# Building both layers' filter spectra before the first layer, keeping them in HBM, and reloading them

## The chip, the cores and the metric

One Trainium2 chip (trn2), one core. TensorE multiplies (PE in the profile, PEld its weight loads), VectorE (DVE), ScalarE (ACT) and GpSimd (POOL) do the element-wise work, SyncE (SP) issues most DMAs. The metric is the device time of one execution in microseconds; lower is better.

## The reference, cut to what matters

Two layers, each over 128 context tokens and 512 latent tokens, model width 1024. Each layer mixes tokens by attention and by a long convolution whose filter is made by a small network from position features only:

```python
def hyena_filters(L, lp):
    ...
    h = jnp.sin(lp['filt_freq1'] * (feats @ lp['filt_w1'] + lp['filt_b1']))
    h = jnp.sin(lp['filt_freq2'] * (h @ lp['filt_w2'] + lp['filt_b2']))
    h = (h @ lp['filt_w3']).reshape(L, 2, HY_W)
    return h * window[:, None, :]

def bidir_long_conv(u, h, bias):
    ...
    G = jnp.fft.rfft(g, n=2 * L, axis=0)      # g: the filter, both halves
    y = jnp.fft.irfft(U * G[None], n=2 * L, axis=1)[:, :L]
    return y + u * bias
```

The filter h, and so its spectrum G, depends on the weights alone, not on the tokens. HY_W is 512. After this branch come two gated projections, an output projection, a LayerNorm and a gated feed-forward network.

## The kernel before

**Arithmetic.** Every large product is made of three matmuls of rounded parts: a float32 operand is split into a high part (a copy to fp32r on ScalarE) and a low part (the difference, on VectorE, sometimes on GpSimd), and high*high, high*low and low*high are added in PSUM. "hi" and "lo" in names mean these parts.

**Weights.** SyncE streams them in chunks of up to 128x2048 through two raw buffers (`stream`, the SyncE program L414 to L449). ScalarE makes `w_hi` (L917) and VectorE `w_lo` (L1312) of each chunk. A chunk's DMA starts once the chunk two places earlier has been split. Chunks named F0, F1, I0, I1 are the blocks of the forward and inverse discrete Fourier transforms. Each engine has its own program, run in the order in which it is written; semaphores tie them.

**Prologue** (before layer 0's first product at L563). `ada` (L455) multiplies the conditioning by eight chunks of `ada` weights, in 16 tiles of 128 columns; ScalarE copies the rows out (L891) and TensorE turns them (L494). TensorE turns the input x into columns (L477), and VectorE copies them out (L1253, L1254). The first two filter-network products run (L485, L497); between them VectorE reduces the argument of the sine (`sine_arg`, L1257 to L1271) and ScalarE takes the sine (L898). The second sine's arguments are worked out in layer 0, between the splits of the q, k and v weights. Then ScalarE and GpSimd make the modulated input h and its two parts for each of eight blocks (`h_make` L964, `h_lo` L1772), and TensorE's `opening` (L549, matmul L563) consumes them as they come: first with the first weight chunk, then (L563 again) with the second.

**Layers.** In both layers: q, k, v; rotary; six z chunks interleaved with attention for five token blocks (`qk` L613, `tpv` L628 and L637). VectorE's `o_sb` (L1415) of the fifth block ends the attention. Then comes the filter and spectrum stage, in this order on TensorE:

1. `u_transposed` for four blocks (L653).
2. Ten filter rows (L759): h2T times w3. VectorE multiplies each by its window (L1541), and for each pair of rows adds and subtracts (L1547, L1548), waits for ScalarE's high part (L921), makes the low part itself (L1316), and only then goes on. Four further sums and differences follow (L1557), each with its parts. GpSimd loads the windows in four pieces (L1814).
3. The filter's spectrum: five pairs, `spectrum` (L668) into `aux_psum`, ScalarE copying to `g_spec` (L1082). Pairs 0, 1 and 2 take 12 matmuls each, pairs 3 and 4 take 24.
4. The signal's spectrum for pairs 0 to 2 (L668 into `gemm_psum`), from u blocks copied by ScalarE (L1072), folded by VectorE (L1564) and split.
5. For each pair VectorE multiplies the two spectra (L1577 to L1592) and splits the result (L1316); `inverse` (L680) starts with pair 1, and pairs 3 and 4 alternate with it.

The chunk of F1 is loaded twice per layer, once for step 3 and once for step 5.

## Time and profile before

| | us |
|---|---|
| Median of the runs shown | 2186.02 |
| Lowest and highest of three | 2185.12, 2197.18 |
| The profiled execution | 2192.11 |
| Its span, first to last instruction | 2190.3 |
| TensorE busy | 2066.8 (94% of the span) |
| VectorE busy | 1171.1 (53%) |
| ScalarE busy | 756.8 (35%) |
| GpSimd busy | 167.5 (8%) |

The span is what the trace covers; 1.8 us lie around it. Busy shares are means over stages with different limits. The chain of waits follows the last instruction back to what released it; a row of it is time that the end of the run depended on. The granted clock is the share of full speed that TensorE's clock had: 1.00 is 2.4 GHz and 0.50 is 1.2 GHz.

### The profile page before, as it was taken

Reading aid. Unit: us, or ns where it says so; the run is one execution under the profiler, and the core shown is the slowest. Engines: PE = TensorE matmul, PEld = TensorE weight load, DVE = VectorE, ACT = ScalarE, POOL = GpSimd, SP = SyncE. Lnnn points to the kernel's source line nnn. Section 1 sums busy time; section 2 is a strip of 40 time slices with the busy share of each in tenths; the row PEclk is TensorE's granted clock in tenths of the full one; section 3 lists DMA queues with packets and bytes.
Section 4 is the critical chain, followed back from the end, with each engine's and each line's share of the span. In section 5 each row is a group of like instructions: output and inputs, shape, how many; then the busy total and the mean of one; then the engine's idle time right before and its main releaser. Section 6 shows DMA issues by size and latency. Waiting matters only on the chain.

```text
span 2190.3 us, 30937 instructions
## 1 busy us (share of the span) xinstructions
PE 2066.8 (94%) x13302; PEld 1968.8 (90%) x13302; DVE 1171.1 (53%) x1716; ACT 756.8 (35%) x1114; POOL 167.5 (8%) x183
## 2 busy tenths in 40 slices
PE   7899978999999999999999997899999999999997
PEld 5888857899989999999988885689998999999996
DVE  3353567765566767776454446772335533234335
ACT  1543424522254321333153243452224533123313
POOL 0300000100032000000130000010003300000011
PEclk9999888999999999999999899899999999999999
DMA  6211021343313345433212012111221221222121
GB/s 241 107 68 39 18 87 49 116 139 141 135 58 112 136 151 181 156 141 142 99 53 95 34 37 87 39 61 66 87 77 61 75 77 54 92 77 77 60 67 49
DMA packets 32721, 199.37 MB, mean 91 GB/s; under 512 B 3926, under 2 KB 4487, under 8 KB 14280
## 3 DMA queue, kind: packets, MB, share of 16 engines
q1 hardware_dynamic: 30424, 188.23, 24.2%
q0 software_dynamic: 2160, 9.16, 1.2%
q8 instruction: 105, 1.72, 0.3%
q14 instruction: 32, 0.26, 0.0%
HBM read 194.49 MB, written 2.88 MB: 90 GB/s over the span
## 4 chain that ended last, share of the span: by engine, by line
PE 84%; DVE 7%; ACT 4%; issue 2%; DMA 1%; SPq 0%; POOL 0%; ACTq 0%; DVEq 0%; POOLq 0%
PE gemm_psum L513 49%; PE gemm_psum L543 14%; PE aux_psum L628 3%; PE gemm_psum L563 3%; PE gemm_psum L526 3%; PE gemm_psum L581 3%; PE aux_psum L680 2%; PE aux_psum L613 2%; PE gemm_psum L668 1%; PE aux_psum L668 1%; ACT h_src_rows L969 1%; PE aux_psum L637 1%; PE gemm_psum L460 1%; ACT w_hi L917 1%; DVE w_lo L1312 1%
## 5 line engine op out<-in xcount | busy, mean ns | idle before, releaser
L513 PE MATMUL gemm_psum<-h_hi,w_hi 128*128 128x322 f32 x2176 | 505.3, 313 | 9.5 <-DVE gates L1636 3.9
L513 PE MATMUL gemm_psum<-h_hi,w_lo 128*128 128x322 f32 x2176 | 502.1, 312 | 0.0
L513 PE MATMUL gemm_psum<-h_lo,w_hi 128*128 128x322 f32 x2176 | 501.1, 311 | 0.0
L1312 DVE TENSOR_TENSOR w_lo<-w_raw,w_hi 128x2048 fp32r<-128x2048 f32 (+3 forms) x146 | 292.2, 2002 | 283.8 <-ACT w_hi L917 282.1
L513 PEld LDWEIGHTS gemm_psum<-h_hi,w_hi 128*128 128x128 f32 x2176 | 369.0, 190 | 15.4 <-issue 10.7
L513 PEld LDWEIGHTS gemm_psum<-h_lo,w_hi 128*128 128x128 f32 x2176 | 369.3, 190 | 0.0
L513 PEld LDWEIGHTS gemm_psum<-h_hi,w_lo 128*128 128x128 f32 x2176 | 368.9, 190 | 0.0
L917 ACT ACTIVATE w_hi<-w_raw 128x2048 fp32r<-128x2048 f32 (+3 forms) x146 | 243.3, 1667 | 160.7 <-PE gemm_psum L543 65.6
L1300 DVE CUSTOM_DVE_ANT_0 aux_psum<-w_raw,cond_by_row 128x1024 f32<-128x1024 f32 x160 | 191.0, 1255 | 7.0 <-DMA w_raw<-in_ada_t 6.9
L1429 DVE SCALAR_TENSOR_TENSOR x<-gemm_psum,mod,x 128x128 f32<-128x128 f32 (+2 forms) x144 | 55.2, 434 | 163.4 <-PE gemm_psum L543 129.9
L543 PE MATMUL gemm_psum<-act_hi,w_lo 128*128 128x322 f32 x616 | 141.9, 311 | 0.0
L543 PE MATMUL gemm_psum<-act_lo,w_hi 128*128 128x322 f32 x616 | 141.5, 311 | 0.0
L543 PE MATMUL gemm_psum<-act_hi,w_hi 128*128 128x322 f32 x616 | 141.5, 311 | 0.0
L1338 DVE SCALAR_TENSOR_TENSOR gate_acc<-gate_rows,par,gate_acc 128x642 f32<-128x642 f32 x88 | 80.8, 919 | 78.1 <-ACT gate_acc L977 76.5
L1500 DVE TENSOR_TENSOR gate_acc<-gate_acc,gemm_psum 128x644 f32<-128x644 f32 x40 | 33.0, 825 | 144.9 <-PE gemm_psum L513 144.9
L543 PEld LDWEIGHTS gemm_psum<-act_hi,w_hi 128*128 128x128 f32 x616 | 104.2, 189 | 0.0
L543 PEld LDWEIGHTS gemm_psum<-act_hi,w_lo 128*128 128x128 f32 x616 | 104.2, 189 | 0.0
L543 PEld LDWEIGHTS gemm_psum<-act_lo,w_hi 128*128 128x128 f32 x616 | 103.9, 189 | 0.0
L563 PE MATMUL gemm_psum<-h_hi,w_hi 128*128 128x322 f32 x224 | 73.9, 330 | 15.4 <-DVE w_lo L1312 10.7
L921 ACT ACTIVATE act_hi<-gate_acc 128x644 fp32r<-128x644 f32 x44 | 32.7, 742 | 157.0 <-DVE gate_acc L1500 148.3
L976 ACT ACTIVATE gate_rows<-gemm_psum 128x644 f32<-128x644 f32 (+1 forms) x48 | 31.8, 663 | 144.0 <-PE gemm_psum L513 142.2
L1401 DVE COPY p_t<-aux_psum 128x384 f32<-128x384 f32 (+2 forms) x40 | 22.3, 558 | 105.9 <-PE aux_psum L637 105.9
(298 smaller groups left out, 3278.5 us busy)
## 6 DMA issues: line engine op xcount, KB each, us to landing
w_raw<-in_w_up SPq DMA_DIRECT2D x44, 1024.0 KB, 4.9
w_raw<-in_ada_t SPq DMA_DIRECT2D x40, 1024.0 KB, 4.7
w_raw<-in_w_down SPq DMA_DIRECT2D x32, 704.0 KB, 4.2
w_raw<-in_w_gate SPq DMA_DIRECT2D x16, 1024.0 KB, 4.7
w_raw<-in_w_z SPq DMA_DIRECT2D x12, 1024.0 KB, 4.7
w_raw<-in_ada SPq DMA_DIRECT2D x8, 1024.0 KB, 6.5
w_raw<-in_w_proj SPq DMA_DIRECT2D x16, 512.0 KB, 3.4
w_raw<-in_w_out SPq DMA_DIRECT2D x8, 1024.0 KB, 4.8
```

Of the source, the lines that this page charges most:

```text
L513: last = mm(gp[:, 2 * (t % 2) + hf, 0:HALF], w[:, off + P * kk:off + P * (kk + 1)], moving(kk, lo)[:, hf * HALF:(hf + 1) * HALF], start=kk ...
L526: last = mm(gp[:, 2 * (t % 2) + hf, 0:HALF], w[:, off + P * kk:off + P * (kk + 1)], moving(kk, lo)[:, half(hf)], start=kk == 0 and n == 0, ...
L543: last = mm(gp[:, 2 * (t % 2) + hf, 0:HALF], w[:, off + P * kk:off + P * (kk + 1)], moving(kk, lo)[:, half(hf)], start=kk == 0 and n == 0, ...
L563: last = mm(banks(c, p_, hf), w[:, P * (KD * c + kk):P * (KD * c + kk + 1)], (hlo if lo else hhi)[:, kk, half(hf)], start=kk == 0 and n == ...
L581: last = mm(gp[:, 2 * ((t0 + c) % 2) + hf, 0:HALF], w[:, P * (KD * c + kk):P * (KD * c + kk + 1)], moving(kk, lo)[:, hf * HALF:(hf + 1) * ...
L613: last = mm(ax[:, n % 4, at:at + P * m], q[pr, j, tok(b)], rhs, start=True, stop=True)
L628: last = mm(ax[:, 2, HD * n:HD * (n + 1)], pt[:, n % 2, P * kb:P * (kb + 1)], v[:, HD * (n % 2):HD * (n % 2 + 1)], start=kb == 0, stop=kb ...
L917: run(whi[s][:, 0:n], raw[st_ % 2][:, 0:n], ACT.Copy).then_inc(sem["w_hi"], raised("w_hi"))
L1300: V.tensor_tensor_reduce(out=ax[:, 2 * gr:2 * gr + 2, :].rearrange("p a b -> p (a b)"), in0=raw[n % 2][:, D_MODEL * (t % 2):D_MODEL * (t % ...
L1312: TT(wlo[s][:, 0:n], raw[STEP[(lane.layer, "g", g)] % 2][:, 0:n], f32(whi[s][:, 0:n]), ALU.subtract).then_inc(sem["w_split"], raised("w_sp ...
L1338: STT(acc[:, 1:ROW - 1], z[:, a:a + ROW - 2], w(tap), acc[:, 1:ROW - 1], ALU.mult, ALU.add).then_inc(sem[event if tap else "dve_order"], r ...
L1429: STT(x[:, m, a:b], gp[:, 2 * (t % 2) + h, a - HALF * h:b - HALF * h], mod[:, gate + m, gr:gr + 1], x[:, m, a:b], ALU.mult, ALU.add)\
```

## The change

- **Where the filter chain runs.** All of it (sine arguments, filter rows, window products, sums and differences, parts, spectra), for both layers, is now in the prologue. The spectra go through a staging buffer `gst` to an HBM tensor `g_kept`, by ten DMAs of 512 KB that ScalarE issues. In each layer GpSimd issues two loads into `g_spec`, after the last `pv` matmul.
- **Streams.** F1 and F0 are loaded once more, as the first two chunks of all (`pre`), and split into the same buffers. Each layer loads F1 once instead of twice; its order is F0, I0, F1, I1. x, w3, all ten windows, the mask, `rot` and `ones` are now loaded by nine DMAs at the head of ScalarE's queue.
- **Who does what.** The low parts of the folded filter blocks (20 of 128x512) go from VectorE to GpSimd. The copies of x go from VectorE to ScalarE. The mask's cast goes to GpSimd. `ada` works in four groups of 512 columns, two chunks each.
- **Layer stage.** After the attention: `u_transposed` for all five blocks, signal spectra, products, inverse. The parts of the last four u blocks are made after pair 0's product.

(In order: `GEMM` and `stream`; TensorE in the prologue and in the layer stage; ScalarE likewise; VectorE in the prologue; GpSimd in the prologue and in the layer. `GSP_PAIRS` is [0, 3, 4, 1, 2]; `TT` is `tensor_tensor`.)

```diff
-        + [("F", 1), ("F", 0), ("I", 0), ("F", 1), ("I", 1)]
+        + [("F", 0), ("I", 0), ("F", 1), ("I", 1)]
...
-    order = [(0, "ada", s) for s in range(ADA_FIRST)]
+    order = [(0, "pre", 1), (0, "pre", 0)] + [(0, "ada", s) for s in range(ADA_FIRST)]
...
+        def g_spectrum(l, pair_):
+            at = GSP_PAIRS.index(pair_)
+            pe.wait_ge(sem["gs_ready"], 10 * l + (2, 6, 6, 10, 10)[at])
+            for o in range(2):
+                r = 10 * l + 2 * at + o
+                if r >= 2:
+                    pe.wait_ge(sem["gsp_out"], r - 1)
...
+                        last = mm(gp[:, 2 + r % 2, :], w[s][:, cols_], v[:, pl, :],
...
+        for n in range(2):
+            mlp(0, n)
+        pe.wait_ge(sem["x_in"], 16 * 3)
+        for d in range(4):
+            x_columns(d)
+        mlp(0, 2)
+        for d in range(4, KD):
+            x_columns(d)
+        for n in range(3):
+            mlp(1, n)
...
+        ada(0)
...
+        filter_rows(0, 0, 4)
+        ada(1)
+        filter_rows(0, 4, 7)
+        ada(2)
+        filter_rows(0, 7, 10)
+        pe.wait_ge(sem["pre_split"], 2)
+        g_spectrum(0, 0)
+        ada(3)
+        g_spectrum(0, 3)
+        ada(4)
+        filter_rows(1, 0, 4)
+        g_spectrum(0, 4)
+        ada(5)
+        g_spectrum(0, 1)
+        filter_rows(1, 4, 7)
+        ada(6)
+        g_spectrum(0, 2)
+        filter_rows(1, 7, 10)
+        ada(7)
+        pe.wait_ge(sem["row_first"], 4)
+        for t in range(2 * KD):
+            tr(gp[:, 0, 2 * t:2 * t + 2], rows0[0:2, P * t:P * (t + 1)], ident[0:2, 0:2]).then_inc(sem["col_mm"], 1)
+        for pair_ in GSP_PAIRS:
+            g_spectrum(1, pair_)
...
+            pe.wait_ge(sem["pt_dve"], due("pt_dve", 20))
+            u_transposed(4)
...
+                pe.wait_ge(sem["us_ready"], due("us_ready", 1 + 2 * p_))
+                pe.wait_ge(sem["ut_out"], due("ut_out", (2, 4, 4)[p_]))
+                spectrum(p_, U_V[p_])
...
+        act.dma_start(xin[:, 0, :], A["x_prompt"][0]).then_inc(sem["x_in"], 16)
...
+        def g_rows(l, r0, r1):
+            for r in range(r0, r1):
+                act.wait_ge(sem["gsp_mm"], 10 * l + r + 1)
...
+                run(gst[:, pair_, r % 2, :], gp[:, 2 + r % 2, :], ACT.Copy).then_inc(sem["gsp_out"], 1)
+                if r % 2:
+                    act.wait_ge(sem["gsp_out"], 10 * l + r + 1)
+                    act.dma_start(g_kept[l, :, pair_], gst[:, pair_]).then_inc(sem["g_spill"], 16)
...
+        sine(2)
+        pre_split(1)
+        sine(3)
+        sine(4)
+        pre_split(0)
+        sine(5)
+        filter_hi(0, 0, 2)
+        first_row(0)
+        filter_hi(0, 2, 6)
+        g_rows(0, 0, 2)
+        first_row(1)
+        filter_hi(0, 6, 10)
+        g_rows(0, 2, 6)
+        filter_hi(1, 0, 2)
+        first_row(2)
+        g_rows(0, 6, 8)
+        filter_hi(1, 2, 4)
+        g_rows(0, 8, 10)
+        filter_hi(1, 4, 6)
+        first_row(3)
+        filter_hi(1, 6, 10)
+        g_rows(1, 0, 6)
...
                 for d in range(KD):
                     h_make(0, 0, d, SH1, SC1)
+                    if d < 4:
+                        g_rows(1, 6 + d, 7 + d)
+                    if d == 1:
+                        split(0)
...
+            u_block(0)
+            u_hi(0, 1)
+            for b in range(1, NB):
+                u_block(b)
+            u_hi(1, 5)
...
+        def filter_blocks(l):
+            for n in range(10):
+                i = 10 * l + n
+                dve.wait_ge(sem["filt_mm"], i + 1)
+                TT(fprod[:, n % 2, :], ax[:, i % 4, :], win[:, n, :], ALU.mult).then_inc(sem["filt_out"], 1)
+                if n % 2 == 0:
+                    continue
...
+                TT(ssum[:, max(n // 2 - 1, 0), :], fprod[:, 0, :], fprod[:, 1, :], ALU.add)\
+                    .then_inc(sem["gs_src" if n == 1 else "filt_order"], 1)
+                TT(dreg[:, :], fprod[:, 0, :], fprod[:, 1, :], ALU.subtract).then_inc(sem["gs_src"], 1)
+                if n < 9:
+                    dve.wait_ge(sem["gs_ready"], 10 * l + n // 2 + 2)
...
+            for n in range(4):
...
+                if n == 2:
+                    dve.wait_ge(sem["gs_ready"], 10 * l + 7)
+                if n == 3:
+                    dve.wait_ge(sem["gs_ready"], 10 * l + 8)
+                TT(fprod[:, n % 2, :], ssum[:, a, :], ssum[:, b, :], op).then_inc(sem["gs_src"], 1)
...
         for n in range(3):
             sine_arg(0, n)
+        pre_split(1)
+        for n in range(2):
+            sine_arg(1, n)
+        pre_split(0)
+        sine_arg(1, 2)
...
+            if l:
+                dve.wait_ge(sem["gs_ready"], 10)
+            filter_blocks(l)
...
+                pool.wait_ge(sem["mlp_arg"], 6)
                 zero_pads([hsrc], "pads_h")
+                for l in range(DEPTH):
+                    for n, v in enumerate(GS_V):
+                        src = ssum[:, 0, :] if n == 0 else dreg[:, :] if n < 6 else fprod[:, n % 2, :]
+                        pool.wait_ge(sem["gs_hi"], 10 * l + n + 1)
+                        G.tensor_tensor(vlo0[:, v, :], src, f32(vhi0[:, v, :]), ALU.subtract).then_inc(sem["gs_ready"], 1)
...
+            pool.wait_ge(sem["pv_mm"], due("pv_mm", 40))
...
+            pool.dma_start(gsp[:, 0:2], g_kept[L, :, 0:2]).then_inc(sem["g_first_in"], 16)
+            pool.dma_start(gsp[:, 2:PAIRS], g_kept[L, :, 2:PAIRS]).then_inc(sem["g_rest_in"], 16)
```

## Rows read from the trace of the kernel before

**Rows 1.** The page, part 4: shares of the chain that ended last.

```profile
PE 84%; DVE 7%; ACT 4%; issue 2%; DMA 1%; SPq 0%; POOL 0%; ACTq 0%; DVEq 0%; POOLq 0%
```

**Rows 2.** Chain of waits, layer 0, filter and spectrum stage (start us, us, what).

```profile
288.28 0.70 DVE o_sb L1415
...
337.21 2.83 PE gemm_psum L668 x12
...
348.27 0.69 DVE prod L1577
...
353.94 0.69 DVE y_lo L1316
...
355.72 8.56 PE aux_psum L680 x24
```

**Rows 3.** Chain of waits, the same stage in layer 1.

```profile
1345.45 0.70 DVE o_sb L1415
...
1412.87 7.47 PE aux_psum L680 x24
```

**Rows 4.** VectorE timeline, layer 0 (start us, us, engine line op out<-in xcount).

```profile
298.10 1.29 DVE L1541 TENSOR_TENSOR prod<-aux_psum,filter_blocks 128x512 f32<-128x512 f32 x2
...
302.14 1.29 DVE L1541 TENSOR_TENSOR prod<-aux_psum,filter_blocks 128x512 f32<-128x512 f32 x2
...
324.50 2.50 DVE L1564 TENSOR_TENSOR u_fold<-u_blocks 128x512 f32<-128x512 f32 x4 [1.81 <-ACT u_blocks L1072]
```

**Rows 5.** TensorE timeline, the first 80 us.

```profile
15.61 1.31 PE L477 MATMUL aux_psum<-ident,x_in 128*128 128x128 f32 x10 [0.31 <-DMA x_in<-in_x_sample]
...
26.50 3.65 PE L460 MATMUL gemm_psum<-w_raw,cs 128*2 128x128 f32 x32
...
71.72 0.64 PE L563 MATMUL gemm_psum<-h_hi,w_hi 128*128 128x322 f32 x1 [2.02 <-DVE w_lo L1312]
```

**Rows 6.** VectorE timeline, the first 80 us.

```profile
31.25 0.81 DVE L1262 TENSOR_SCALAR h1T<-gemm_psum,mlp_vec 128x512 f32<-128x512 f32 x1 [0.26 <-PE gemm_psum L485]
...
35.53 0.54 DVE L1262 TENSOR_SCALAR h1T<-aux_psum,mlp_vec 128x256 f32<-128x256 f32 x1
...
38.14 0.29 DVE L1271 TENSOR_SCALAR h1T<-h1T 128x256 f32<-128x256 f32 x1
...
69.37 2.29 DVE L1312 TENSOR_TENSOR w_lo<-w_raw,w_hi 128x2048 fp32r<-128x2048 f32 x1 [10.68 <-ACT w_hi L917]
```

**Rows 7.** Instruction groups by form (busy us, mean ns | idle us before them).

```profile
L917 ACT ACTIVATE w_hi<-w_raw 128x2048 fp32r<-128x2048 f32 x92 | 175.1, 1903 | 45.1 <-DMA w_raw<-in_w_up 17.7 <-PE gemm_psum L543 16.4 <-PE gemm_psum L513 9.0
...
L1082 ACT ACTIVATE g_spec<-aux_psum 128x512 f32<-128x512 f32 x20 | 11.3, 608 | 5.7 <-PE aux_psum L668 5.7
...
L1776 POOL TENSOR_TENSOR h_lo<-h_src_rows,h_hi 128x322 fp32r<-128x322 f32 x64 | 60.1, 940 | 110.4 <-ACT h_hi L972 110.3
...
L1786 POOL TENSOR_TENSOR sums<-x 128x644 f32<-128x644 f32 x4 | 6.3, 1577 | 794.1 <-DVE x L1429 794.1
```

**Rows 8.** SyncE queue timeline, layer 0: one weight DMA issued.

```profile
293.99 0.33 SPq L443 DMA_DIRECT2D w_raw<-in_F  x1
```

**Rows 9.** GpSimd timeline, the first 110 us.

```profile
70.46 2.76 POOL L1776 TENSOR_TENSOR h_lo<-h_src_rows,h_hi 128x322 fp32r<-128x322 f32 x2 [1.96 <-ACT h_hi L972]
```

**Rows 10.** Stretches, TensorE alone: us, busy (x), granted clock, DMA share, GB/s.

```profile
0.00:59.60 59.60, 43.91 (x325) 0.97 0.66 238
...
200.00:220.00 20.00, 18.81 (x112) 0.70 0.15 53
...
300.00:320.00 20.00, 10.68 (x25) 0.66 0.17 53
```

**Rows 11.** TensorE timeline, 80 to 135 us: its only wait there.

```profile
96.43 0.53 PE L513 MATMUL gemm_psum<-h_hi,w_hi 128*128 128x322 f32 x2 [1.68 <-ACT q L997]
```

**Rows 12.** ScalarE timeline, making h for layer 0.

```profile
56.73 0.93 ACT L969 ACTIVATE h_src_rows<-x,mod 128x128 f32<-128x128 f32 x2 [0.36 <-PE aux_psum L497]
...
66.11 0.92 ACT L969 ACTIVATE h_src_rows<-x,mod 128x128 f32<-128x128 f32 x2
```

More of the change, by code:

```diff
@@ L436, in _ @@
                     sp.wait_ge(sem["w_split"], NG * before[0] + CREDIT["w_split"] + before[2] + 1)
-            if what == "ada":
+            if what == "pre":
+                src, w = A[f"F{i}"], (F0_BLOCKS, F1_BLOCKS)[i] * P
+            elif what == "ada":
                 src, w = A["ada"][i] if L == 0 and i < ADA_FIRST else A["ada_t"][L, i], CHUNK
@@ L478, in _ @@
             last.then_inc(sem["x_tr"], 1)
-        cols = [(0, 512), (512, 1024), (1024, NT)]
-        pe.wait_ge(sem["consts_in"], 16 * 7)
-        for n, (a, b) in enumerate(cols):
-            if n == 2:
-                pe.wait_ge(sem["x_row"], 16)
-            mm(mlp_bank(0, n)[:, 0:b - a], w1[:, :], feat[:, a:b], start=True, stop=True).then_inc(sem["mlp_mm"], 1)
-            for t in range(4 + 2 * n, 6 + 2 * n):
-                pe.wait_ge(sem["row_first"], t - 1)
-                ada(t)
@@ L489, in _, with mlp @@
-        for t in range(10, 4 * ADA_GROUP):
-            pe.wait_ge(sem["row_first"], t - 1)
-            ada(t)
-        for t in range(4 * ADA_GROUP):
-            pe.wait_ge(sem["row_first"], t + 1)
-            tr(ax[:, 3, 2 * t:2 * t + 2], rows0[0:2, t, :], ident[0:2, 0:2]).then_inc(sem["col_mm"], 1)
-        for n, (a, b) in enumerate(cols):
-            pe.wait_ge(sem["mlp_sin"], n + 1)
-            mm(mlp_bank(1, n)[:, 0:b - a], w2[:, :], h1T[:, a:b], start=True, stop=True).then_inc(sem["mlp_mm"], 1)
+        def mlp(lay, n):
+            a, b = ((0, 512), (512, 1024), (1024, NT))[n]
+            i = 3 * lay + n
+            if i >= 2:
+                pe.wait_ge(sem["mlp_arg"], i - 1)
+            if lay:
+                pe.wait_ge(sem["mlp_sin"], n + 1)
+            mm(mlp_bank(lay, n)[:, 0:b - a], (w1, w2)[lay][:, :], (feat, h1T)[lay][:, a:b], start=True, stop=True)\
+                .then_inc(sem["mlp_mm"], 1)
@@ L701, in q_free @@
             def q_free(hf, p_):
+                if L == 0 and hf == 0:
+                    pe.wait_ge(sem["gsp_out"], 20)
                 if hf:
@@ L898, in sine @@
             run(dst[:, a:b], dst[:, a:b], ACT.Sin).then_inc(sem["mlp_sin"], 1)
-        first_rows(0, 6)
-        for i in range(3):
-            first_rows(6 + 2 * i, 8 + 2 * i)
-            sine(i)
-        first_rows(12, 16)
+        act.wait_ge(sem["x_zero"], 3)
+        for d in range(3):
+            x_rows(d)
+        sine(0)
+        for d in range(3, 6):
+            x_rows(d)
+        sine(1)
+        for d in range(6, KD):
+            x_rows(d)
+        sine(2)
[20 more added lines that the diff above has]
+        g_rows(1, 0, 6)
         def split(g):
@@ L1025, in _ @@
                 q_half(t, 1)
+            split(4)
             if L == 0:
-                sine(4)
-            split(4)
+                act.wait_ge(sem["g_spill"], 16 * PAIRS * DEPTH)
             for t in range(4, 6):
@@ L1564, in _ @@
                 TT(ufold[:, n, :], ureg[:, a, :], ureg[:, b, :], op).then_inc(sem["us_src"], raised("us_src"))
-            for n in range(9):
-                if n == 4:
-                    split(gF + 2)
-                src = ureg[:, n, :] if n < 4 else uctx[:, :] if n == 4 else ufold[:, n - 5, :]
-                if n == 5:
-                    dve.wait_ge(sem["us_src"], now("us_src"))
-                lo(vlo[:, US_V[n], :], src, vhi[:, US_V[n], :], "us_hi", n + 1, "us_ready")
+            dve.wait_ge(sem["us_src"], now("us_src"))
+            u_lo(1, 5)
             for p_ in range(PAIRS):
@@ L1996, in _layouts @@
     w_ada = np.asarray(i["w_ada"])
-    out["ada"] = chunks(w_ada[:1, :, :2 * D_MODEL], 2)[0]
+    first = w_ada[0, :, :2 * D_MODEL].reshape(2, 4, P, 4, 512)
+    out["ada"] = np.ascontiguousarray(first.transpose(3, 0, 2, 1, 4)).reshape(ADA_FIRST, P, CHUNK)
     w_t = w_ada.transpose(0, 2, 1).reshape(D, ADA_STEPS, 2, P, D_MODEL)
```

349 lines of the change are left out of this document (172 added, 177 removed).

## The prediction

> **What bounds the kernel now.** I read the page first: TensorE is on 84% of the chain that ended last [rows 1]. What the change can win is time in which TensorE waits, so I read the chain of waits in the filter and spectrum stage. In layer 0 the attention ends when `o_sb` ends, at 288.28 + 0.70 = 288.98. The signal's first spectrum starts only at 337.21, and the first inverse at 355.72 [rows 2]. Between 289 and 337 the reader sees one VectorE sequence repeated every 4.04 us (the pair of products at 298.10, the next at 302.14 [rows 4]). Layer 1 is the same: 1346.15 to 1412.87 [rows 3]. So from the attention's end to the first inverse it is 66.7 us in each layer, most of it work that needs no token. In the prologue TensorE's second group of `opening` matmuls starts at 71.72 [rows 5]. I use three marks: that one, the attention's end, and the first inverse. Behind the first inverse the order of work stays as it was, at the same distances.
>
> **What leaves the layers.** Marks from the attention's end, for the changed kernel, along its longest chain:
>
> - Turning the o rows 0.7 and their high part 0.6; ScalarE's high part of I0 1.9 [rows 7]; VectorE's low part 2.3 [rows 6]: 5.5.
> - Low part of the context block 0.7, four folds 2.6, four low parts 2.5 (four operations of this size take 2.50 [rows 4]): 5.8, sum 11.3. TensorE's first spectrum (2.8) and ScalarE's copies end just before this.
> - Product of pair 0: as pair 1 took before, from 348.27 to 353.94 + 0.69, 6.4 [rows 2]. Sum 17.7.
> - Four low parts that are now behind pair 0: 2.5. Pair 1: 6.4. Context part 1.1 (354.63 to 355.72 [rows 2]). Sum 27.7.
>
> Each layer wins 66.7 - 27.7 = 39.0, two win 78.0. The reload must land before the product of pair 0, 11 us after the attention; its first part is 1 MB, a weight chunk's size, and it is issued at the last `pv`; I take it as hidden. The sine arguments in layer 0 also go. Their only effect that TensorE saw is one wait of 1.68 [rows 11]. Won: 79.7.
>
> **What the prologue costs.** TensorE, ScalarE, VectorE and GpSimd now hand each block round, so I add up the longest chain in order. The times are estimates from the rows named.
>
> 1. x lands at about 14.6 (before at 15.6 [rows 5]; it is now ahead of ScalarE's other loads and shares the engines with the F chunks). Eight column groups at 1.1 each (TensorE 0.66 at full clock, 1.3 at half, from 10 transposes in 1.31 [rows 5]): 23.4. Sine 0.4, high part of F1 1.9, low part 2.3: 28.0. VectorE is idle for some 4 us ahead of this split, since ScalarE is behind the copies of x.
> 2. Two sine arguments of 512 columns, 4.3 each (31.25 to 35.53 [rows 6]): 36.6. Sine 0.6, F0's parts 1.7 + 2.0: 40.9. The last argument 2.9 (35.53 to 38.43 [rows 6]), sine 0.4, first filter row 0.9 (32 matmuls of 128 columns take 3.65 [rows 5], a row is eight times 128), waits between 0.1: 45.2.
> 3. **Low parts on GpSimd.** No row shows 128x512. 322 columns take 0.94 and 644 take 1.58 on average [rows 7]; the line through both gives 1.3 at 512. Bounds: 0.69, what VectorE takes, and 2.2, from the two of 322 columns that took 2.76 while VectorE made a low part [rows 9, 6]. I take 1.3: in this chain VectorE mostly stands still meanwhile. The Trainium skill, GPSIMD Engine Reference, section 4.1, states that a two-input elementwise operation is about 2 times slower on GpSimd and says to use VectorE; by it one takes 1.4 and the sum grows by some 2 us.
> 4. Layer 0's blocks. Pair of rows one: products 1.3, sum and difference 1.3, high part 0.6, two low parts 2.6: 5.7 with overlap. Pairs two to four: 1.3 + 1.3 + 0.6 + 1.3 + 0.2 = 4.7 each (it was 4.04): 14.1. Pair five 2.6: 67.6. Then high part 0.6, a fold that holds GpSimd off 0.7, low part 1.3, 0.1: the sixth part is ready at 70.3.
> 5. Now TensorE's order counts. Spectrum of pair 3, 24 matmuls at 0.236 (12 in 2.83 [rows 2]): 5.7. `ada` chunk 3.65. Four filter rows of layer 1: 3.6. Spectrum of pair 4: 5.7. That is 89.0. ScalarE copies it (0.6), issues its DMA (0.3 by SyncE's issue [rows 8]), and only then comes to layer 1's first high part, though that block was done near 83. High part 0.6, two low parts 2.6, 0.2: 93.3.
> 6. Layer 1's pairs two to five: 5.0, 4.7, 6.1 (a filter row waits behind `ada` and a spectrum), 2.6: 111.7. Folds: 0.7 + 0.7, three low parts 3.9, fold 0.7, two high parts 1.2: 118.9.
> 7. ScalarE copies layer 1's first spectrum only after these: 0.6, and TensorE had two banks, so it stood. Four blocks of 12 matmuls 11.3, copy and issue 1.0: 131.8.
> 8. Only then h is made: seven blocks took 9.4 (56.73 to 66.11 [rows 12]), so eight take 10.7. Inside are now four copies 2.4, two issues 0.6, the first weight's high part 1.9: 147.4. Second weight 1.9 + 2.3: 151.6, or 151.7 with the handover.
> 9. TensorE starts from a wait at 70.3 and at 119.5. Such a start cost 2.9 at 355.72: 24 matmuls in 8.56 instead of 5.7 [rows 2]. I take half of it twice, 2.8 (bounds 0 and 5.8).
>
> The mark moves from 71.7 to 151.7 + 2.8 = 154.5, by 82.8. Sum: 82.8 - 79.7 = 3.1 us longer. The profiled execution would go from 2192.1 to 2195.2. The median lay 6.1 below that execution, so the median goes to 2186.0 + 3.1 = 2189; I say **2190**.
>
> Hidden work: spilling 5 MB and the six MB of extra loads (the prologue's share of the DMA engines was 0.66 [rows 10] while less was hidden; ten spills of 512 KB are spread over 60 us). If a queue stalls ScalarE at the head, x is copied later and all of step 1 moves: 0 to 4 us. GpSimd's mask cast is behind nothing that waits.
>
> **The rivals.**
>
> - **A. The two sides cancel** (my forecast, 0.66). For it: the sums above. The chain is serial on both sides, so moving it hides little. Its own range is 2170 to 2210: without the half-clock starts, with the low parts at VectorE's 0.69 on the 18 that lie on the chain (-10) and x 2.5 earlier it is 2190 - 2.8 - 10 - 2.5 - 4 (issues at nothing) = 2171; with low parts at 1.7 (+7), a stalled queue (+4), the starts in full (+3) and the reload late by 5 it is 2209.
> - **B. TensorE at half clock through the prologue** (slower by over 1%, 0.22). Steps 5 and 7 hold 18.7 + 11.3 = 30 us of TensorE on the chain. If the granted clock is 0.5 there, they take 60: 2190 + 30 = 2220. It decides from 19 us, two thirds of that stretch at half clock. For: in the filter stage, where TensorE also did little between waits, the clock was 0.66, and 0.70 in one attention stretch where it was busy with small matmuls [rows 10]. Against: 0.97 over the old prologue, busy 43.91 of 59.60 [rows 10]. The Trainium skill, TensorE: Matmul & The Clock Gate, Part 1, states that the clock falls to 1.2 GHz after idleness and that how many matmuls run cold varies from run to run; by that rule the waits of steps 5 and 7 could each bring such a stretch, which is B again.
> - **C. The blocks flow faster than I add** (faster by over 1%, 0.12). Layer 1's chain would have to begin near 70 instead of 83, beside TensorE's spectra, and ScalarE's copies would have to be free when TensorE ends. Then steps 5 to 7 shrink to layer 1's own 33 us behind 78: 2190 - 20 = 2170, and with A's cheap low parts (-10) 2160. It decides when the mark of 154.5 falls under 132. Against: the order written for ScalarE and TensorE.
> - **D. The reload is late.** A wait at the first product in each layer. Its price is the lateness twice; from 8 us each it makes the time slower by over 1%. A 1 MB load against a window of 11 us makes that unlikely; it is inside A's range and counted with B.
>
> **How the numbers follow.** About 1% (22 us) is what a measurement of this kernel can tell from no change. Faster by over 1% is C: 0.12. Slower is B and the tail of D: 0.22. Within 1%: 0.66. The range should leave out 2 in 10: 2168 takes in A's low end and a part of C; 2217 takes in A's high end and nearly all of B's price.
>
> **What would show it.** Right: the second group of `opening` starts between 145 and 165; the attention's end to the first inverse is 27 to 29 us in both layers; VectorE's product pairs in the prologue stand 4.7 apart; ScalarE's first high part of layer 1 comes after 88 and follows a copy of a spectrum. Wrong: that mark under 135 (C), a granted clock of 0.5 over most of 70 to 130 (B), `L1577` waiting for a DMA in the layers (D), or GpSimd's low parts far from 1.3.

## The result, and the profile after

The changed kernel takes 2197.75 us (median of 17 runs) where the kernel before takes 2190.28 in the same runs: a ratio of 1.0037, with an interval of 1.0019 to 1.0055, so about 8 us (4 to 12) longer. That is within 1%, as forecast, on the slow side. (One of the 17 runs took 2626.61 us at a mean granted clock of 0.72; the ratio leaves it out.) The profiled executions go from a span of 2190.3 to 2195.9 us, 5.6 longer. The sum had said 3.1.

The shares of the chain that ended last, of the changed kernel, hardly differ from [rows 1]: the change trades one stage for another.

```profile
PE 85%; DVE 7%; ACT 4%; issue 2%; POOL 1%; DMA 1%; SPq 0%; ACTq 0%; DVEq 0%; POOLq 0%
```

**The layers.** The chain of waits of the changed kernel (start us, us, what), layer 0 and layer 1, beside [rows 2, 3]:

```profile
368.52 0.70 DVE o_sb L1555
...
375.55 5.47 PE gemm_psum L729 x12
...
381.68 0.69 DVE prod L1698
...
396.03 0.69 DVE y_lo L1456
...
397.82 7.48 PE aux_psum L741 x24
```
```profile
1389.56 0.70 DVE o_sb L1555
...
1417.60 7.86 PE aux_psum L741 x24
```

From the attention's end to the first inverse it is 397.82 - 369.22 = 28.6 us in layer 0 and 27.3 in layer 1, where it was 66.7 in both. VectorE's timeline of the changed kernel shows what the first product with the reloaded spectrum waited for:

```profile
378.02 2.50 DVE L1456 TENSOR_TENSOR v_lo<-u_fold,v_hi 128x512 fp32r<-128x512 f32 x4
381.68 0.69 DVE L1698 TENSOR_TENSOR prod<-u_spec,g_spec 128x512 f32<-128x512 f32 x1 [1.16 <-ACT u_spec L1201]
```

It waited for ScalarE's copy of the signal's spectrum, not for a DMA. That copy was late because TensorE's first spectrum, the row at 375.55, ran at half clock: 5.47 us for the 12 matmuls that the forecast put at 2.8. In layer 1 the product had no wait and started 11.2 us after the attention's end, as the forecast has it; this is the difference between 28.6 and 27.3. The reload (issued at 369.03, first part landed 5.4 us later) is hidden in both.

**The prologue.** TensorE's timeline of the changed kernel (start us, us, engine line op out<-in xcount, in brackets the idle time before it and what ended it). L477 turns x, L498 makes filter rows, L467 is ada, L514 the filter's spectra, L555 turns the rows of ada, L624 is `opening`, for the first token products:

```profile
18.36 4.49 PE L477 MATMUL aux_psum<-ident,x_in 128*128 128x128 f32 x20 [3.37 <-DMA ident<-in_ident]
```
```profile
48.12 6.23 PE L498 MATMUL aux_psum<-w,h2T 128*128 128x512 f32 x8 [6.05 <-issue]
...
75.77 0.50 PE L514 MATMUL gemm_psum<-filter_hi,w_hi 128*128 128x512 f32 x1 [2.49 <-POOL filter_lo L1926]
...
77.77 0.63 PE L514 MATMUL gemm_psum<-filter_lo,w_hi 128*128 128x512 f32 x1
...
83.10 3.59 PE L467 MATMUL gemm_psum<-w_raw,cs 128*2 128x512 f32 x8
...
120.34 1.17 PE L555 MATMUL gemm_psum<-ident,mod_rows_first 2*128 2x2 f32 x16 [2.66 <-ACT mod_rows_first L947]
...
121.95 0.63 PE L514 MATMUL gemm_psum<-filter_lo,w_hi 128*128 128x512 f32 x1
```
```profile
149.23 0.60 PE L624 MATMUL gemm_psum<-h_hi,w_hi 128*128 128x322 f32 x1 [4.53 <-ACT g_rows_out L971]
...
158.98 0.42 PE L624 MATMUL gemm_psum<-h_hi,w_hi 128*128 128x322 f32 x1 [1.05 <-DVE w_lo L1452]
```

The second group of `opening` starts at 158.98, where it stood at 71.72 [rows 5]: 87.3 us later. And windows of the changed kernel, the first from the first filter row to the end of the last spectrum (stretch, its us, then busy time of PE, PEld, DVE, ACT and POOL, PE's granted clock, DMA share, GB/s):

```profile
48.00:144.70 96.70, 90.38 (x280) 46.84 (x280) 33.59 (x52) 28.16 (x50) 27.97 (x22) 0.94 0.37 138
70.00:80.00 10.00, 7.51 (x21) 3.84 (x20) 6.14 (x8) 3.71 (x7) 4.84 (x4) 0.86 0.42 157
120.00:130.00 10.00, 9.14 (x43) 7.24 (x44) 3.08 (x7) 3.87 (x8) 6.67 (x5) 0.83 0.30 126
240.00:260.00 20.00, 20.00 (x116) 18.40 (x117) 12.70 (x29) 8.77 (x21) 0.00 (x0) 0.80 0.03 6
```

In the first row TensorE is busy for 90.4 of 96.7 us. VectorE is busy for 33.6, a third. The other rows are stretches with a lowered granted clock. One more is short and lower still: 0.58 from 48.0 to 54.3, the first four filter rows, behind the 6.05 us of idleness.

The 5.6 us add up by marks: 87.3 lost in the prologue; 7.0 gained between that mark and the attention's end of layer 0 (217.3 us before, 210.2 after: the wait of 1.68 [rows 11] is gone, and the kernel before had a clock of 0.70 in a stretch of that part [rows 10], where 0.80 is now the lowest; this distance differs from profile to profile, see below); 38.1 and 39.4 gained in the two layers; 2.8 lost in all the rest. 87.3 - 7.0 - 38.1 - 39.4 + 2.8 = 5.6.

### The profile page after: what moved, and what is told of

It reads as the page before. It is cut to its first block, busy times and chain, and to the rows that moved or that the text cites. A ratio compares the mean times of both kernels' runs of the same rounds, so it can differ in the third digit from the quotient of the medians.

```text
span 2195.9 us, 30546 instructions
## 1 busy us (share of the span) xinstructions
PE 2069.6 (94%) x13110; PEld 1955.1 (89%) x13110; DVE 1151.3 (52%) x1679; ACT 761.1 (35%) x1118; POOL 187.7 (9%) x200
## 4 chain that ended last, share of the span: by engine, by line
PE 85%; DVE 7%; ACT 4%; issue 2%; POOL 1%; DMA 1%; SPq 0%; ACTq 0%; DVEq 0%; POOLq 0%
PE gemm_psum L574 49%; PE gemm_psum L604 14%; PE gemm_psum L624 3%; PE aux_psum L689 3%; PE gemm_psum L642 3%; PE gemm_psum L587 2%; PE aux_psum L674 2%; PE aux_psum L741 2%; PE gemm_psum L514 1%; PE gemm_psum L729 1%; PE aux_psum L698 1%; ACT h_src_rows L1080 1%; ACT w_hi L1028 1%; PE gemm_psum L467 1%; DMA ident<-in_ident 1%
## 5 line engine op out<-in xcount | busy, mean ns | idle before, releaser
L1452 DVE TENSOR_TENSOR w_lo<-w_raw,w_hi 128x2048 fp32r<-128x2048 f32 (+2 forms) x144 | 287.7, 1998 | 306.4 <-ACT w_hi L1028 304.8
L1028 ACT ACTIVATE w_hi<-w_raw 128x2048 fp32r<-128x2048 f32 (+2 forms) x144 | 239.6, 1664 | 170.1 <-PE gemm_psum L604 65.6
L624 PE MATMUL gemm_psum<-h_hi,w_hi 128*128 128x322 f32 x224 | 74.2, 331 | 15.5 <-DVE w_lo L1452 9.9
```

What stands on the lines that cost most here:

```text
L624: last = mm(banks(c, p_, hf), w[:, P * (KD * c + kk):P * (KD * c + kk + 1)], (hlo if lo else hhi)[:, kk, half(hf)], start=kk == 0 and n == ...
L1028: run(whi[s][:, 0:n], raw[st_ % 2][:, 0:n], ACT.Copy).then_inc(sem["w_hi"], raised("w_hi"))
L1452: TT(wlo[s][:, 0:n], raw[STEP[(lane.layer, "g", g)] % 2][:, 0:n], f32(whi[s][:, 0:n]), ALU.subtract).then_inc(sem["w_split"], raised("w_sp ...
```

## The experiments

The marks of all kernels, in us from the start of the span. The last columns are the profiled span and the ratio to the kernel before, measured in the same runs, with its interval.

| Kernel | First filter row | `opening`, first group | Second group | Attention's end, layer 0 | Span | Ratio |
|---|---|---|---|---|---|---|
| before | - | - | 71.7 | 289.0 | 2190.3 | 1 |
| changed | 48.1 | 149.2 | 159.0 | 369.2 | 2195.9 | 1.0037 (1.0019 to 1.0055) |
| e1 low parts on VectorE | 48.5 | 143.9 | 153.7 | 364.0 | 2185.5 | 0.9995 (0.9972 to 1.0017) |
| e2 identity first | 46.0 | 147.2 | 156.9 | 375.5 | 2207.8 | 1.0033 (1.0007 to 1.0059) |
| e3 h early | 48.2 | 147.5 | 156.2 | 362.7 | 2178.7 | 0.9999 (0.9978 to 1.0019) |
| e6 layer 1 early | 48.1 | 145.0 | 154.7 | 359.9 | 2176.0 | 0.9976 (0.9954 to 0.9998) |
| e4 one layer | 49.6 | 120.0 | 130.3 | 343.1 | 2160.3 | 0.9869 (0.9835 to 0.9903) |
| e7 splits late | 39.7 | 142.2 | 151.9 | 362.1 | 2179.2 | 1.0000 (0.9978 to 1.0022) |
| e8 order | 47.9 | 140.0 | 149.8 | 359.7 | 2181.5 | 0.9978 (0.9957 to 0.9999) |
| e9 all edits | 37.6 | 129.1 | 136.3 | 346.1 | 2160.9 | 0.9918 (0.9886 to 0.9949) |
| e10 all, GpSimd | 38.1 | 129.6 | 136.8 | 347.0 | 2163.7 | 0.9931 (0.9901 to 0.9960) |
| e11 all, no third product | 38.1 | 124.0 | 131.1 | 346.5 | 2172.8 | 0.9913 (0.9893 to 0.9933) |
| e12 all again | 38.4 | 129.9 | 137.1 | 343.7 | 2173.3 | 0.9945 (0.9926 to 0.9964) |

Read the marks first. Behind the attention's end of layer 0 all kernels from the changed one on execute the same instructions (e4 with layer 0's spectra in place of layer 1's, so its time is not that of a kernel that does the whole work). Yet that rest took from 1814.8 us (e9) to 1832.3 us (e2). The longest goes with the lowest mean granted clock of TensorE (0.966 in e2; 0.981 in e9). A spread of 17 us in one execution is more than any of the single edits from e1 to e8 moves the mark (e4, which leaves work out, apart), so a span or a median tells less of an edit in the prologue than the mark behind it. The distance from the second group to the attention's end varies too, from 205.2 (e6) to 218.6 us (e2), so the attention's end is no substitute for that mark. The mark itself differs by 0.8 us between the two profiles of one kernel, e9 and e12.

**e1: low parts back on VectorE.**

```diff
 # GpSimd: the loop over GS_V with its twenty subtractions is taken out
+def filter_lo(l, n):                                   # VectorE
+    dve.wait_ge(sem["gs_hi"], 10 * l + n + 1)
+    TT(vlo0[:, GS_V[n], :], src, f32(vhi0[:, GS_V[n], :]), ALU.subtract)...
```

> The changed kernel with the twenty low parts of the folded filter blocks made by VectorE instead of GpSimd, nothing else. Marks of the changed kernel: layer 0's sixth part lets TensorE's next spectrum start at 75.8 us, layer 1's first spectrum starts at 121.4, the second group of opening starts at 159.0. Theory T (from the first filter row at 48 us on TensorE's own queue is full, with only 2.5 + 2.7 us of waits for blocks up to 139 us): the pairs come 4.0 instead of 4.66 us apart, but only those two waits can be won, so the last mark comes 3 to 6 us earlier, and the time is 3 to 6 us under that of the changed kernel. Theory S (the serial chain of my sum: VectorE, ScalarE and GpSimd hand each block round and eighteen low parts lie on it): 18 times 0.57 us, the mark and the time about 10 us earlier.

Measured: the second group moves by 5.3 us (theory T), not by 10 (theory S). GpSimd's row in the changed kernel and VectorE's in e1, for the same operation:

```profile
59.95 1.26 POOL L1926 TENSOR_TENSOR filter_lo<-d_block,filter_hi 128x512 fp32r<-128x512 f32 x1 [3.39 <-ACT filter_hi L962]
...
73.93 1.78 POOL L1926 TENSOR_TENSOR filter_lo<-d_block,filter_hi 128x512 fp32r<-128x512 f32 x1 [3.39 <-ACT filter_hi L962]
```
```profile
59.24 0.69 DVE L1384 TENSOR_TENSOR filter_lo<-d_block,filter_hi 128x512 fp32r<-128x512 f32 x1 [0.86 <-ACT filter_hi L962]
...
63.28 0.69 DVE L1384 TENSOR_TENSOR filter_lo<-d_block,filter_hi 128x512 fp32r<-128x512 f32 x1 [0.69 <-ACT filter_hi L962]
```

One costs 1.26 against 0.69 us, and the low parts come 4.04 apart (59.24, 63.28) instead of 4.66. The 0.57 us on each is as I had it; that all eighteen lie on the path is what fails. The ratio fell by 0.0042, 9 us, more than the mark moved; the rest behind the attention's end was 5 us shorter in this profile too, with the same instructions, so I read the mark.

**e2: identity first.**

```diff
+sp.dma_start(ident[:, :], A["ident"])...               # first on SyncE's queue
 for dst, src in ((w1, "w1"), (feat, "feat"), (mlpv, "mlpv"), (w2, "w2")):
...
-    if n == 1:                                         # it stood behind F1 (1 MB)
-        sp.dma_start(ident[:, :], A["ident"])...
```

> The changed kernel with the DMA of the identity (64 KB) issued first on SyncE's queue instead of behind the 1 MB of F1, nothing else. In the changed kernel TensorE waited for it until 18.36 us. Theory I (the identity is what was late, and the chain of the prologue begins with the columns of x): columns of x start at 15 us, where the first two matmuls of the filter's network end, F1's low part ends at 29 instead of 31.9 us, and the last mark (159.0) and the time come 2 to 3.5 us earlier. Rival: x itself is late or the gain is used up by the waits behind; then less than 1 us.

Measured: TensorE's columns of x in e2 start at once behind the filter network's product, as this row shows by having no wait:

```profile
15.34 4.65 PE L476 MATMUL aux_psum<-ident,x_in 128*128 128x128 f32 x20
```

The 64 KB landed 2.2 us after their issue, against 14.7 in the changed kernel, and x was there. F1's low part ends at 29.8 instead of 31.9, and the first filter row and the last mark both come 2.1 us earlier. So the identity was what delayed step 1. The ratio does not show it: this profile has the longest rest of all.

**e3: h beside layer 1's spectra.**

```diff
 filter_hi(1, 6, 10)                                    # ScalarE
-g_rows(1, 0, 6)
...
-act.wait_ge(sem["gs_ready"], 20)
...
 for d in range(KD):
     h_make(0, 0, d, SH1, SC1)
-    if d < 4: g_rows(1, 6 + d, 7 + d)
-    if d == 1: split(0)
+split(0)
 split(1)
+# the five DMAs of g_kept; VectorE makes the ten copies of g_rows(1, ...)
```

> The changed kernel with ScalarE making the eight blocks of h (first half) right after layer 1's last high part at 126 us, beside layer 1's spectra, instead of after them; VectorE, which is idle there, copies layer 1's spectra out of PSUM, and ScalarE issues their five DMAs after the two weights' high parts. Nothing is computed differently. Theory T (TensorE's queue is the bound up to its last spectrum): the spectra end at about 143.7 us as TensorE's work allows, both weights are split by 148, the first group of opening starts at once and takes 7.3 us, so the second group starts at about 151 instead of 159.0, and the time falls by 8 us. Rival: ScalarE's blocks of h were not what was late (GpSimd's low parts or the DMA of the second weight are): less than 2 us.

Measured: the first group starts 1.8 us earlier, the second 2.8. The forecast of 8 failed, and the rival said less than 2. h was no longer what was late, but two other things were: VectorE's low part of the first weight stood behind its own ten copies, a wait of 3.03 us, and behind that wait TensorE fell to half clock, matmuls of 322 columns 0.27 instead of 0.15 us apart from 148.5 to 151.7:

```profile
147.47 0.39 PE L624 MATMUL gemm_psum<-h_hi,w_hi 128*128 128x322 f32 x1 [3.03 <-DVE w_lo L1450]
...
150.88 0.47 PE L624 MATMUL gemm_psum<-h_hi,w_hi 128*128 128x322 f32 x1
```

The attention's end comes 6.5 us earlier, but only 2.8 of these lie ahead of the mark. What h off the path is worth shows in e9: from the end of the last spectrum to the second group it is 8.0 us there, and 14.3 in the changed kernel.

**e6: layer 1 earlier, first try.**

```diff
 ada(3)                                                 # TensorE
+filter_rows(1, 0, 4)
 g_spectrum(0, 3)
-ada(4)
-filter_rows(1, 0, 4)
 g_spectrum(0, 4)
+ada(4)
...
-g_rows(0, 2, 6)                                        # ScalarE
-filter_hi(1, 0, 2)
+g_rows(0, 2, 4)
+filter_hi(1, 0, 2)
+g_rows(0, 4, 6)
```

> The changed kernel with three moves in the written orders: TensorE makes layer 1's first four filter rows ahead of layer 0's spectrum of pair 3 (in the gap where it waited 2.5 us), the ada chunk between the spectra of pairs 3 and 4 goes behind both, and ScalarE makes layer 1's first two high parts ahead of the copies of pair 4. VectorE's second pair of layer 1 should then come at 90 us instead of 100.3. Theory S (the chain of blocks sets the end): the mark of 159.0 and the time 8 to 10 us earlier. Theory T (TensorE's queue is full): only its waits of 2.5 and 2.7 us and the half-clock stretches behind them can be won, 3 to 6 us, and the profile shows TensorE without a wait over 1 us from 50 to 139 us.

Measured: 4.3 us, theory T's size, but this run does not decide. ScalarE's written order stalled the chain again one block later. VectorE of e6, the second and the third pair of layer 1:

```profile
88.12 1.29 DVE L1386 TENSOR_TENSOR filter_prod<-aux_psum,windows 128x512 f32<-128x512 f32 x2 [2.72 <-POOL filter_lo L1927]
...
101.29 1.29 DVE L1386 TENSOR_TENSOR filter_prod<-aux_psum,windows 128x512 f32<-128x512 f32 x2 [10.55 <-POOL filter_lo L1927]
```

The second pair came at 88.1 as intended, and the third waited 10.55 us, because ScalarE's high part stood behind a row of ada and two copies (its timeline puts it at 99.29). A wait behind in-order work moves to the next instruction unless every instruction of the group is moved.

**e8: the whole order.** TensorE: ada(3), rows (1, 0 to 3), spectra of pairs 3 and 4, rows (1, 4 and 5), ada(4), rows (1, 6 and 7), spectrum 1, rows (1, 8 and 9), ada(5), spectrum 2, ada(6), ada(7). ScalarE:

```diff
-g_rows(0, 2, 6); filter_hi(1, 0, 2); first_row(2); g_rows(0, 6, 8)
-filter_hi(1, 2, 4); g_rows(0, 8, 10); filter_hi(1, 4, 6); first_row(3); filter_hi(1, 6, 10)
+g_rows(0, 2, 4); filter_hi(1, 0, 2); g_rows(0, 4, 6); filter_hi(1, 2, 4); g_rows(0, 6, 8)
+filter_hi(1, 4, 5); first_row(2); filter_hi(1, 5, 6); g_rows(0, 8, 10); filter_hi(1, 6, 10); first_row(3)
```

> The changed kernel with a written order in which nothing of layer 1 waits for a copy of layer 0 that is not needed: TensorE makes layer 1's rows 0 to 3 ahead of layer 0's spectra of pairs 3 and 4, which then follow each other, and the other rows two by two between single ada chunks and spectra; ScalarE takes each high part of layer 1 ahead of the copy or the row of ada that would come later. The last experiment on the order moved ScalarE's stall only from layer 1's first high part to its third (VectorE then waited 10.6 us at 101 us). Now layer 1's pairs should come from 83 us on 5 us apart, its sixth part at about 108 instead of 121. Theory S (the chain of blocks sets the end): mark and time 12 us earlier. Theory T (TensorE's queue is full): TensorE's work from 73 us to its last spectrum is about 61 us at full clock, so the last spectrum ends at 135 to 137 instead of 143.7, the mark 7 to 9 us earlier, with no wait of TensorE over 1 us from 50 to 135.

Measured: this one decides. VectorE's pairs of layer 1 now run through, 5.3 and then 4.7 apart, and its last folds start at 108.89 instead of 122.93:

```profile
82.62 1.29 DVE L1388 TENSOR_TENSOR filter_prod<-aux_psum,windows 128x512 f32<-128x512 f32 x2 [2.72 <-POOL filter_lo L1929]
...
87.95 1.29 DVE L1388 TENSOR_TENSOR filter_prod<-aux_psum,windows 128x512 f32<-128x512 f32 x2 [2.71 <-POOL filter_lo L1929]
...
92.61 1.29 DVE L1388 TENSOR_TENSOR filter_prod<-aux_psum,windows 128x512 f32<-128x512 f32 x2 [2.04 <-POOL filter_lo L1929]
...
108.89 2.34 DVE L1405 TENSOR_TENSOR filter_prod<-filter_sums 128x512 f32<-128x512 f32 x2 [2.93 <-POOL filter_lo L1929]
```

The blocks are 14.0 us earlier, but the mark only 9.2. TensorE's queue is what is left, in the row from its first filter row to its last spectrum:

```profile
48.00:135.50 87.50, 86.27 (x280) 44.52 (x280) 33.50 (x52) 28.49 (x49) 27.99 (x22) 0.98 0.41 151
```

It is busy 86.3 of 87.5 us. Of the 9.2 us that e8 won, 5.1 are idle time of TensorE (6.3 us in the changed kernel's window, 1.2 here: the wait of 2.49 is gone and the one of 2.66 is down to 0.68), and 4.1 are busy time, mostly the matmuls at half clock behind the two waits.

**e7: both low parts of F behind the sine arguments.**

```diff
-pre_split(1)                                           # VectorE
-for n in range(2):
+for n in range(3):
     sine_arg(1, n)
-pre_split(0)
-sine_arg(1, 2)
+pre_split(1)
+pre_split(0)
```

> The changed kernel with VectorE making all six sine arguments before the low parts of F1 and F0 (ScalarE makes both high parts early, TensorE the first four filter rows ahead of the first ada chunk). Nothing else. The last sine argument ends at about 43 instead of 47.6 us, the first filter row starts at 44 instead of 48.1, the two low parts follow and the first product comes at 47 to 48 instead of 50.3. Theory T (TensorE's queue is full from its first filter row on, so what counts is when that row starts): the mark of 159.0 comes about 3 to 4 us earlier. Rival: the ada chunks, whose buffers come free only with the two low parts, arrive later, TensorE waits for them and nothing is won, or up to 3 us lost.

Measured: the first filter row starts 8.4 us earlier and the mark comes 7.1 us earlier. My forecast of the row was 4 too late: not only the two low parts (4.3 us) leave the sine chain, but also VectorE's waits for their high parts (3.17 and 2.28). The rule of theory T holds: the mark follows the start of TensorE's first row, less a short wait for the ada chunk (0.89):

```profile
39.73 5.49 PE L498 MATMUL aux_psum<-w,h2T 128*128 128x512 f32 x8 [7.05 <-ACT h2T L981]
46.11 7.03 PE L467 MATMUL gemm_psum<-w_raw,cs 128*2 128x512 f32 x16 [0.89 <-DMA w_raw<-in_ada]
```

**e4: one layer only.** It leaves out layer 1's rows, blocks, spectra and spills; layer 1 reloads `g_kept[0]`.

> The changed kernel with layer 1's filter chain left out of the prologue (its ten filter rows, folded blocks, low parts, spectra and spills); layer 1 loads layer 0's spectra instead, so layer 1's filter is the wrong one, and the time is that of a kernel which prepares one layer only. It prices the two halves of what the prologue took over, against 39 us won in each layer. Theory T (TensorE's queue is the bound): without 9.2 us of rows and 20 us of spectra, and with the half-clock start, the second group of opening moves from 159.0 to about 126 us: layer 1 costs 33 us and wins 39, layer 0 costs 55 and wins 39. Theory S (the chain of blocks, step 5 to 7 of my sum): layer 1 costs 40 to 42 us, the mark comes at 118. Time of the changed kernel less 33 (T) or less 41 (S).

Measured: the mark falls by 28.7, to 130.3. So preparing one layer costs 58.6 us in the prologue, against 38.1 or 39.4 won, and the second layer adds 28.7 and wins as much again. The second one pays; the first does not. This split depends on the order of counting: the 58.6 hold the start that either layer would need (F1 and F0, the sine arguments), and a kernel that prepares layer 1 alone was not built. Theory T's 33 was 4 too high: the first row came 1.5 later in this profile, and h and the weights took 17.8 us behind TensorE's last work before `opening` (112.4 to 130.3) instead of 14.3 (144.7 to 159.0). Theory S's 41 is far off.

**e9 to e12: all edits.** e9 joins e1, e2, e7, e8 and e3, with ScalarE making the last four copies between the two weights, and one filter-network product moved ahead of x's fourth column group. e12 is e9 again. e10 puts the low parts back on GpSimd. e11 leaves out the third product in layer 0's last four spectra:

```diff
-for n, (w, v) in enumerate(((whi, vhi0), (whi, vlo0), (wlo, vhi0))):
+terms = ((whi, vhi0), (whi, vlo0), (wlo, vhi0))[:2 if l == 0 and at else 3]
+for n, (w, v) in enumerate(terms):
```

> All edits at once: low parts of the folded filter blocks on VectorE, identity first, the order of the experiment e8, the two splits behind the sine arguments, and h made beside layer 1's spectra (VectorE copies the first six of them, ScalarE the rest, between the two weights). Nothing is computed differently. Theory T: TensorE's queue starts some 6 us earlier (first filter row at 40 to 42 us), loses its waits (5 to 7 us) and is followed by h at once (8 us): the second group of opening at 138 to 141 instead of 159.0, the time 18 to 21 us under the changed kernel and 10 to 14 us under the kernel before, a ratio of 0.994 to 0.995. Rival: the edits compete for VectorE and ScalarE, and the mark stays above 146: a ratio of 0.997 or more.

> The kernel with all edits (e9), but with the twenty low parts back on GpSimd, as in the changed kernel. In e9 TensorE was busy 89.1 of the 91 us from its first filter row (37.6) to its last spectrum, and the second group of opening started at 136.5. Theory T (TensorE's queue is the bound, the blocks come early enough either way): pairs 4.66 instead of 4.04 us apart, yet the mark within 2 us of e9's (136 to 138.5) and the time within 2 us. Theory S (the place of the low parts counts by their number on the chain): 18 times 0.57, mark at 146 and time 10 us more than e9.

> The kernel with all edits (e9), but layer 0's spectra of the last four pairs are made without their third product (the weight's low part times the block's high part): 24 matmuls of 0.236 us less on TensorE, no other engine does less, and layer 0's filter loses that part of its accuracy. Theory T: the mark comes 5.7 us earlier, at 131, and the time is 5.7 us less than e9's. Theory S (VectorE and ScalarE with their blocks are last): less than 1.5 us.

> The kernel with all edits (e9) once more, unchanged, beside its two variants, because TensorE's granted clock behind the prologue differs from run to run. The mark of the second group of opening at 136.5 again within 0.5 us. Time under the kernel before: theory T, by the marks (159.0 - 136.5 = 22.5 us under the changed kernel, which stood 8 us over the kernel before), 14 us, a ratio of 0.9935; e9 measured 0.9918 with an interval from 0.9886 to 0.9949, so between 0.991 and 0.995. Rival: e9's gain was the luck of the clock, then 0.996 or more.

Measured: the second group at 136.3 (e9) and 137.1 (e12), 22 us earlier than in the changed kernel. e9 was forecast at 138 to 141, too late, and e12 within 0.5 us of 136.5, missed by 0.1. TensorE in e12 and e11, the first group of `opening`, with its short wait for a copy:

```profile
129.91 0.38 PE L624 MATMUL gemm_psum<-h_hi,w_hi 128*128 128x322 f32 x1 [0.89 <-ACT g_rows_out L1124]
```
```profile
123.95 0.38 PE L625 MATMUL gemm_psum<-h_hi,w_hi 128*128 128x322 f32 x1 [0.89 <-ACT g_rows_out L1125]
```

Taking 24 x 0.236 = 5.7 us of matmuls from TensorE, and from nothing else, moves the mark by 6.0 (e12 to e11; 5.1 from e9). Giving VectorE's low parts to GpSimd or back moves it by 0.6 or less (e9 or e12 to e10). With the order right, TensorE's queue sets the prologue's length from the first filter row to the last spectrum, shown from both sides. The start of that row is still set by the sine chain: its wait in e12 is for ScalarE's `h2T`. The ratios of e9 and e12 are 0.9918 and 0.9945: both intervals lie below 1, some 12 to 18 us under the kernel before. My forecast for e12 was 0.991 to 0.995, and for e9 0.994 to 0.995, too little gain. The times do not show e11's 5.7 us: its median is 0.7 us under that of e9 and 9.4 under that of e12, and those two are the same kernel.

## Why the prediction was right, and where it was off

- **The layers: right.** 27.7 us forecast from the attention's end to the first inverse, 28.6 and 27.3 measured; 78.0 won forecast, 77.5 measured. The path of the forecast is that of layer 1; in layer 0 TensorE's first spectrum, which I had ending just before VectorE's parts, ran at half clock and cost 1.2 us. Rival D (the reload is late) falls by VectorE's row at 381.68.
- **Step 1: mis-sized.** F1's low part was to end at 28.0 and ended at 31.9. x was in time; the identity, a 64 KB DMA issued behind the 1 MB of F1, was not (e2). I had followed x through the queues, but not the small load that SyncE now issues between two large ones. It is 3.9 of the mark's miss of 4.5; e2 got 2.1 of it back.
- **Step 2: mis-sized.** One filter row 0.9 was at full clock. The first four took 6.23 us after 6.05 us of idleness, instead of 3.6, and the first product came 2.2 us behind the start of the first row. With step 1, it came at 50.3, 5.1 late.
- **Step 3: right.** 1.26 us for a 128x512 low part, forecast 1.3. The Trainium skill, GPSIMD Engine Reference, section 4.1, with its factor of about 2, would give 1.4; the trace has 1.26 / 0.69 = 1.8.
- **Step 4: right.** VectorE's pairs of the changed kernel stand 4.65 apart, forecast 4.7; the sixth part was ready at 75.8, which is 70.3 plus the 5.1 of the start and 0.4 (0.6 more for the first pair, whose second row was at half clock, and 0.2 less for the rest):

```profile
56.59 1.29 DVE L1385 TENSOR_TENSOR filter_prod<-aux_psum,windows 128x512 f32<-128x512 f32 x2 [2.67 <-POOL filter_lo L1926]
...
61.24 1.29 DVE L1385 TENSOR_TENSOR filter_prod<-aux_psum,windows 128x512 f32<-128x512 f32 x2 [2.04 <-POOL filter_lo L1926]
...
100.28 1.29 DVE L1385 TENSOR_TENSOR filter_prod<-aux_psum,windows 128x512 f32<-128x512 f32 x2 [9.61 <-POOL filter_lo L1926]
```

- **Step 5: right as a mechanism.** ScalarE's first high part of layer 1 came at 97.03 (the sign was: after 88), directly behind the copy and the DMA of pair 4's spectrum:

```profile
96.61 0.33 ACTq L974 DMA_DIRECT2D g_kept<-g_rows_out  x1
97.03 0.63 ACT L962 ACTIVATE filter_hi<-filter_sums 128x512 fp32r<-128x512 f32 x1 [0.46 <-ACT g_rows_out L971]
```

  An issue costs ScalarE 0.46 us between a copy and the next activation, where I took 0.3. VectorE stood for 9.61 us ahead of its pair at 100.28, as a result.
- **Steps 6 to 8: right.** Folds done at 126.0 (118.9 forecast), the last split at 158.9 (151.7): both 7.1 or 7.2 late. That is 5.1 of the start, the 0.4, and 1.6 for pair 3's spectrum, which took 7.33 us (75.77 to 83.10) instead of 5.7, in part at half clock. Nothing was added behind step 5.
- **Step 9: right in size, half of it in the wrong place.** I took 2.8 for two half-clock starts. The profile has some eight matmuls 0.43 instead of 0.236 us apart behind the wait at 75.77, and as many behind the one at 120.34, 1.6 us each. Only the first lay on the path. The second was hidden: ScalarE made layer 1's last high parts until 125.96 and copied both rows of the spectrum behind them without a wait. The mark, forecast at 154.5, came at 159.0. Steps 1 to 5 are 7.1 late with the real half-clock start in them, the 2.8 of this step then falls away, and 0.2 are rounding and handover.
- **The sum: partly luck.** The prologue cost 4.5 more than forecast (87.3, not 82.8), the layers won 0.5 less, and all the rest lost 2.8 that I had at nothing. Against this the stretch between the mark and the attention's end of layer 0 was 7.0 shorter, where I had 1.7. In profiles of kernels with the same instructions there it was anything from 5 us shorter to 8 us longer than in the changed kernel's. So 5.6 beside 3.1 is nearer than the terms deserve; the two layers and the mark are what the forecast got right.
- **The difference.** Of the 7.75 us between 2190 and the median, 4.3 are the kernel before itself, 2190.28 in these runs instead of 2186.02. The forecast of the difference was 3.1, the profiles say 5.6, the medians 8 (4 to 12).
- **Rival B did not come, in size.** The granted clock was 0.94 from 48 to 144.7, with 0.86 from 70 to 80 and 0.83 from 120 to 130, around the two waits. TensorE had work nearly all the time, as in the old prologue with its 0.97 [rows 10]. In e8, without the first wait, it was 0.98. The Trainium skill, TensorE: Matmul & The Clock Gate, Part 1, has the clock fall after idleness; the trace agrees, with 2.49 and 2.66 us of it ahead of the two stretches. Both waits stand behind a chunk of `ada`, whose matmuls have weights of two columns. These alone did not lower the clock: in e8 two such chunks, 7.0 us, and a wait of 0.68 us were followed by full clock.
- **What was wrong in how I read the chain.** I added VectorE's, ScalarE's and GpSimd's turns as if each shortened block shortened the prologue: 10 us for cheap low parts in rival A's range, 20 for an earlier layer 1 in rival C. They gave 5.3 (e1) and 9.2 (e8). The blocks and TensorE's queue ended within a few us of each other, so my sum along the blocks came out right for this order of work; that they lay so close was luck. But the floor under both was TensorE's own work, 86 to 90 us from the first row to the last spectrum, and I never added that up. C's condition (a mark under 132) could not be met by the order alone; e9 needed an earlier start and h off the path to reach 136.

## What to carry to other kernels

Work that one engine did while another stood idle is not free once it is moved: add up the busy time of every engine in the stretch that it is moved to, beside the longest chain. Here TensorE's filter work, hidden under VectorE's chain in the layers, became the floor of the prologue. Where two bounds lie within a few us, a cut in one gives back at most the gap to the other; the cuts that counted in every run were an earlier start of the full queue (e2, e7) and, in e9, shorter work behind its end; e3 alone got less than half of that, since its new wait brought a half-clock start. Check small loads as carefully as large ones: 64 KB behind 1 MB on one queue held up the head of the whole chain.
